# Second mixer's gate and branch slabs computed token-major, with 512 moving weight columns

## The chip, the cores and the metric

One core of one Trainium2 chip runs the whole kernel. The metric is the device time in microseconds of one execution, the median of three runs.

## What is computed

Two transformer blocks over 256 tokens of 1024 features, in fp32. The change touches the second block's mixer (`hybrid_mixer`): three branches of width 512 (stick-breaking attention `ya`, spatial gating `yb`, gated short convolution `yc`), each projected to 1024 features and weighted by a sigmoid gate that is itself a projection of the normed input; the weighted sum is projected once more.

```
p = h @ w_in                                   # h is the normed input, (256, 1024)
q, k, v, z, cb, cc, cx, gates = split(p)       # gates: 3 * 1024 columns
br = stack([ya, yb, yc], axis=2)               # (256, 3, 512)
br_d = einsum("bsnc,ncd->bsnd", br, w_branch)  # (256, 3, 1024)
g = sigmoid(gates.reshape(bsz, seq, 3, 1024))
merged = sum(g * br_d, axis=2)                 # (256, 1024)
return merged @ w_out
```

## The kernel before

All weights pass through a ring of four places in SBUF in slabs of 128 x 2048 words (1 MB). SyncE loads slab i when slab i-4 has been used (`slab_used`). Every fp32 product is made of three fp32r matmuls, high by high, high by low and low by high (`mm3`, lines 529 to 531). For this ScalarE copies each slab into `w_hi` (line 1065) and VectorE subtracts that to make `w_lo` (line 1502). Each engine has its own program in a fixed order, and semaphores tie them together. `hi(i)`, `lo(i)` and the waits stand in these programs exactly where they run.

`form_a` is feature-major: a 128x128 block of the weights is stationary, and the 256 tokens of the input move past it. The output has features on partitions and tokens along the free dimension. A slab of 256 columns and 8 blocks of input features takes 48 matmuls of 256 columns. `form_b_half` is token-major: a 128x128 block of the input is stationary and 512 weight columns move. The output has tokens on partitions. A slab of 4 blocks of input features and 512 columns takes 24 matmuls of 512 columns. Both forms are in use in the kernel before.

The mixer's stage takes slabs 87 to 104 in six rounds r = 0 to 5, one for each branch (order `yb`, `yc`, `ya`) and half of the output features. A round has three slabs: two gate slabs and one branch slab. Round 0 is 87, 88 and 89, round 1 is 90, 91 and 92, and so on to 102, 103 and 104. Slabs 105 to 108 are the output projection (`form_b`), which is token-major and takes the merged result as features on partitions, split into `xh` and `xl` (lines 1408 and 2060). The PSUM banks `feat(0)` and `feat(1)` hold the gates, `feat(2)` and `feat(3)` the branch's output.

In a round of the kernel before, TensorE does the first gate slab into `feat(0)` and the second into `feat(1)`. VectorE multiplies each by the tokens' norm scales, which lie along the free dimension (`row_of_scales`, line 2069), into `sig2` in SBUF, and counts `gate_in`. TensorE of the next round waits for `gate_in` before it writes the bank anew. ScalarE makes the sigmoid in place (line 1421, `gate_ready`). After the branch slab VectorE merges: products of PSUM and `sig2` (lines 2088 and 2093) and a sum (line 2094), `merge_done`.

Beside these slabs run the steps of the stick-breaking attention, for four pairs of heads. TensorE does scores (line 917), sums (929 to 931) and values (939, 940) after fixed slabs (`beside`), and ScalarE (lines 1343 to 1355, with Exp and Ln) and VectorE (lines 1941 to 1967) serve them in their own queues (`early`, `beside`). In round 0 ScalarE's order is: exponential of pair 1, `hi` of slabs 90 and 91, the logarithm step of pair 2, and then the two sigmoids. Just before it stand the splits of `yb` and `yc` (lines 1401 and 1403), the latter waiting for VectorE's products at line 2050.

Of the kernel before, what the change touches and what calls it, by code (L numbers as in the profile page):

```python
# [158 lines left out]
def weight_count(i):  # L159

    return i + 1 if i < I_M2 else i


def build(nc, a, out):

    with ExitStack() as ctx:
# [3 lines left out]
        def at(name, shape, off, dt=F32):  # L170
            assert off + int(np.prod(shape[1:])) <= ARENA_WORDS, (name, off)
            return nc.alloc_sbuf_tensor_at(name, shape, dt, offset=ARENA + 4 * off)
# [101 lines left out]
        y3_pad = at("y3_pad", [P, 4, CONV3 - 1 + S], kv0)  # L274
        cc_s = at("cc_s", [P, 2, S], kv0 + 4 * (CONV3 - 1 + S))
        acc3 = at("acc3", [P, 4, S], kv0 + 4 * (CONV3 - 1 + S) + 2 * S)
        merged = at("merged", [P, KD, S], kv0)
        vg = at("vg", [P, TB, HALF], kv0 + 3 * D)
        sig2 = at("sig2", [P, 4, S], kv0 + 3 * D)
        y_h = [at("ya_h", [P, 4, S], xn0, F32R), at("yb_h", [P, 4, S], split0, F32R),  # L280
               at("yc_h", [P, 4, S], split0 + 2 * D, F32R)]
        y_l = [at("ya_l", [P, 4, S], xn0 + D, F32R), at("yb_l", [P, 4, S], split0 + D, F32R),
# [23 lines left out]
        def feat(b):  # L306
            return ps[:, 4 + b, :]

        def blocks(x):
            return x.rearrange("p (t n) -> p t n", n=S)  # L310

        def sem(name):
            return ctx.enter_context(nc.semaphore(name))
# [10 lines left out]
        gain_loaded, gain_used = sem("gain_loaded"), sem("gain_used")  # L324
        raw_t, raw_hi, raw_lo, hg_ready, h_scaled = sem("raw_t"), sem("raw_hi"), sem("raw_lo"), sem("hg_ready"), sem("h_scaled")
        diag_ready, row_t, row_ready = sem("diag_ready"), sem("row_t"), sem("row_ready")
        sig_in, rg_in, ug_in, gate_in, glu_in_ready = (sem(x) for x in ("sig_in", "rg_in", "ug_in", "gate_in", "glu_in_ready"))
        fill, const_ready, tables_ready, dist_set = sem("fill"), sem("const_ready"), sem("tables_ready"), sem("dist_set")
        ws_masked, pad3_ready = sem("ws_masked"), sem("pad3_ready")
        act_step, dve_step = sem("act_step"), sem("dve_step")  # L330
# [37 lines left out]
        def _(sp):  # L368
            def load(i, src, step=0, wait_step=0):

                s = PLACE[i]
                if BEFORE[i] is not None:
                    sp.wait_ge(slab_used, BEFORE[i] + 1 + wait_step)
                dst = w_ring[:, s, :].rearrange("p (k n) -> p k n", n=src.shape[2])
                sp.dma_start(dst, src).then_inc(w_loaded[s], 16)

            def panel_a(w, col, n=256):
                return w.rearrange("(k p) n -> p k n", p=P)[:, :, col:col + n]
# [61 lines left out]
            for n, br in enumerate(BRANCH_ORDER):  # L440
                for half in range(2):
                    i = I_BR + 6 * n + 3 * half
                    for j in range(2):
                        load(i + j, panel_a(w2, 8 * HALF + D * br + HALF * half + 256 * j))
                    load(i + 2, panel_a(wb[br], HALF * half, HALF))
            for j in range(4):
                load(I_OUT2 + j, rows_b_form(a["w_out_2"].squeeze(0), 256 * j))
# [77 lines left out]
        def _(pe):  # L525
# [427 lines left out]
            def beside(i):  # L953

                for step, p in SB_AT.get(i, ()):
                    step(p)
# [28 lines left out]
            mm.then_inc(sgu_mixed, 1)  # L985
            form_a(I_C3 + 5, (3,), x_t)
            beside(I_C3 + 5)
            for n, br in enumerate(BRANCH_ORDER):
                for half in range(2):
                    i = I_BR + 6 * n + 3 * half  # L990
                    r = 2 * n + half
                    if r == 0:
                        pe.wait_ge(yb_ready, 2)
                    for j in range(2):
                        if r > 0:
                            pe.wait_ge(gate_in, 2 * r - 1 + j)
                        form_a(i + j, (j,), x_t)
                        beside(i + j)
                    if r == 0:
                        pe.wait_ge(yc_ready, 2)  # L1000
                    else:
                        pe.wait_ge(merge_done, r)
                    pe.wait_ge((sb_lo, yb_lo, yc_lo)[br], (4, 1, 1)[br])
                    form_a(i + 2, (2, 3), (y_h[br], y_l[br]), n=HALF)
                    beside(i + 2)

            pe.wait_ge(sb_lo, 4)
            form_b(I_OUT2, x_t, range(4), lambda s: pe.wait_ge(merged_lo, 1 + s // 2),
                   lambda: raw_transpose(R_XA2, 0, UPD[I_OUT2]))
            raw_transpose(R_XA2, 1, UPD[I_OUT2])  # L1010
            x_attention(1, I_Q2, I_O2, raw_ready(R_XA2), lambda: raw_transpose(R_FF2, 0, UPD[I_O2]))
# [40 lines left out]
        def _(act):  # L1052
# [316 lines left out]
            def early(i):  # L1369

                for step, p in SB_EARLY.get(i, ()):
                    step(p)

            def beside(i):
                for step, p in SB_AT.get(i, ()):
                    step(p)
# [27 lines left out]

            def merged_split(half):

                act.wait_ge(merge_done, 5 + half)
                act.activation(xh[:, 4 * half:4 * half + 4, :], merged[:, 4 * half:4 * half + 4, :], ACT.Copy).then_inc(merged_hi, 1)

            for n in range(BRANCHES):  # L1410
                for half in range(2):
                    i = I_BR + 6 * n + 3 * half
                    r = 2 * n + half
                    if r == 0:
                        sb_exps(1)
                        hi(i + 3)
                        hi(i + 4)
                        sb_logs(2)
                    for j in range(2):
                        act.wait_ge(gate_in, 2 * r + j + 1)  # L1420
                        act.activation(sig2[:, 2 * j:2 * j + 2, :], sig2[:, 2 * j:2 * j + 2, :], ACT.Sigmoid).then_inc(gate_ready, 1)
                        if 0 < r < 5:
                            early(i + j)
                            hi(i + j + 3)
                            beside(i + j)
                    if r == 5:
                        merged_split(0)
                        hi(i + 3)
                        hi(i + 4)
                    early(i + 2)  # L1430
                    if r < 5:
                        hi(i + 5)
                    beside(i + 2)
# [55 lines left out]
        def _(dve):  # L1489
# [51 lines left out]
            def row_of_scales(n):  # L1541

                return r_row[:, n, :].unsqueeze(1).broadcast_to([P, 2, S])
# [438 lines left out]
            def early(i):  # L1982

                for step, p in SB_EARLY.get(i, ()):
                    step(p)
# [69 lines left out]
            dve.tensor_tensor(y_l[2][:, :, :], acc3[:, :, :], y_h[2][:, :, :].bitcast(F32), ALU.subtract).then_inc(yc_lo, 1)  # L2055

            def merged_split(half):
                dve.wait_ge(merged_hi, half + 1)
                f = slice(4 * half, 4 * half + 4)
                dve.tensor_tensor(xl[:, f, :], merged[:, f, :], xh[:, f, :].bitcast(F32), ALU.subtract).then_inc(merged_lo, 1)  # L2060


            for n in range(BRANCHES):
                for half in range(2):
                    i = I_BR + 6 * n + 3 * half
                    r = 2 * n + half
                    for j in range(2):
                        dve.wait_ge(slab_used, i + j + 1)
                        dve.tensor_tensor(sig2[:, 2 * j:2 * j + 2, :], blocks(feat(j)), row_of_scales(0), ALU.mult).then_inc(gate_in, 1)
                        if 0 < r < 5:  # L2070
                            early(i + j)
                            lo(i + j + 3)
                            beside(i + j)
                    if r == 0:
                        sb_masked(1)
                        lo(i + 3)
                        lo(i + 4)
                        sb_penalty(2)
                    if r == 5:
                        merged_split(0)  # L2080
                        lo(i + 3)
                        lo(i + 4)
                    dve.wait_ge(gate_ready, 2 * r + 2)
                    dve.wait_ge(slab_used, i + 3)
                    m = merged[:, 4 * half:4 * half + 4, :]
                    if n == 0:
                        for j in range(2):
                            ins = dve.tensor_tensor(m[:, 2 * j:2 * j + 2, :], blocks(feat(2 + j)), sig2[:, 2 * j:2 * j + 2, :], ALU.mult)
                            after(ins)
                    else:  # L2090
                        for j in range(2):
                            s2 = sig2[:, 2 * j:2 * j + 2, :]
                            after(dve.tensor_tensor(s2, blocks(feat(2 + j)), s2, ALU.mult))
                        after(dve.tensor_tensor(m, m, sig2[:, :, :], ALU.add))
                    dve.sem_inc(merge_done, 1)
                    early(i + 2)
                    if r < 5:
                        lo(i + 5)
                    beside(i + 2)
# [104 lines left out]
```

## Time and profile before

| what | us |
|---|---|
| median of three runs (lowest to highest) | 943.25 (943.23 to 944.71) |
| the profiled execution | 943.54 |
| its span, first to last instruction | 941.8 |
| TensorE matmul busy | 918.0 |
| TensorE weight load busy | 822.0 |
| VectorE busy | 672.5 |
| ScalarE busy | 486.8 |
| mean granted TensorE clock | 0.997 of full |

The profile is of one execution. Engines are PE (TensorE), PEld (its weight loads), DVE (VectorE), ACT (ScalarE), POOL (GpSimd) and SP (SyncE). Matmul ends are modelled and matmuls overlap, so the distance between starts tells what one costs. In brackets behind a row of a timeline stands the idle time of the engine before it, with what released it.

### The profile page before, as it was taken

What the parts mean: (1) busy time and instruction counts of PE and PEld (TensorE: products, weight loads), DVE (VectorE), ACT (ScalarE), POOL (GpSimd) and SP (SyncE); (2) the same over time, 40 slices, a digit from 0 to 9 for tenths busy, and PEclk for the clock granted to TensorE, in tenths of its full rate; (3) what the DMA queues carried; (4) which work ended last, traced back from release to release, by engine and by line L of the source; (5) the groups of instructions that cost most, each with busy time, mean ns of one, the idle gap of its engine ahead of it and who ended that gap; (6) DMA issues with size and microseconds to landing.
All of it is one profiled execution on the core that took longest, in us unless ns stands there. A gap on an engine that the chain in (4) does not pass through costs nothing.

```text
span 941.8 us, 14045 instructions
## 1 busy us (share of the span) xinstructions
PE 918.0 (97%) x5768; PEld 822.0 (87%) x5768; DVE 672.5 (71%) x964; ACT 486.8 (52%) x554; POOL 6.9 (1%) x37
## 2 busy tenths in 40 slices
PE   6998999999999999999999999999999999999996
PEld 6996999889888888888999999999898888888885
DVE  5799999888576566666866886765786676565665
ACT  6776435475455444445646546653564554544442
POOL 1000000000000000000000000000000000000000
PEclk9999999999999999999999999999999999999998
DMA  9675545454346655654755444545453455556551
GB/s 316 236 232 181 179 135 171 142 179 145 124 143 198 196 178 181 202 196 146 234 180 179 154 157 138 180 157 189 147 179 114 155 179 179 184 197 196 180 179 45
DMA packets 112467, 164.43 MB, mean 175 GB/s; under 512 B 2784, under 2 KB 90464, under 8 KB 112416
## 3 DMA queue, kind: packets, MB, share of 16 engines
q1 hardware_dynamic: 111856, 161.87, 52.6%
q0 software_dynamic: 560, 1.84, 0.6%
q8 instruction: 38, 0.62, 0.3%
q14 instruction: 13, 0.11, 0.0%
HBM read 162.64 MB, written 1.05 MB: 174 GB/s over the span
## 4 chain that ended last, share of the span: by engine, by line
PE 87%; DVE 9%; DMA 2%; ACT 2%; issue 1%; SPq 0%; DVEq 0%
PE ps L529 20%; PE ps L531 20%; PE ps L530 20%; PE ps L572 14%; PE ps L573 7%; DVE w_lo L1502 3%; DMA w_ring<-in_w_in 2%; DVE c_acc L1641 2%; PE ps L660 1%; PE ps L696 0%; ACT w_hi L1065 0%; DVE acc L2040 0%; DVE h L1560 0%; DVE mem_l L1517 0%; ACT c_out L1241 0%
## 5 line engine op out<-in xcount | busy, mean ns | idle before, releaser
L1502 DVE TENSOR_TENSOR w_lo<-w_ring,w_hi 128x2048 fp32r<-128x2048 f32 x147 | 335.5, 2289 | 122.1 <-ACT w_hi L1065 120.2
L1065 ACT ACTIVATE w_hi<-w_ring 128x2048 fp32r<-128x2048 f32 x147 | 279.9, 1908 | 80.0 <-DMA w_ring<-in_w_in 25.9
L572 PE MATMUL ps<-xx,w_hi 128*128 128x512 f32 x576 | 203.9, 398 | 0.3
L529 PE MATMUL ps<-xx,w_hi 128*128 128x256 f32 x616 | 177.3, 288 | 8.9 <-DVE w_lo L1597 8.7
L530 PE MATMUL ps<-xx,w_hi 128*128 128x256 f32 x616 | 175.2, 284 | 0.0
L531 PE MATMUL ps<-xx,w_lo 128*128 128x256 f32 x616 | 175.2, 284 | 0.0
L573 PE MATMUL ps<-xx,w_lo 128*128 128x256 f32 x576 | 161.6, 280 | 0.0
L572 PEld LDWEIGHTS ps<-xx,w_hi 128*128 128x128 f32 x576 | 108.2, 188 | 27.0 <-issue 0.7
L529 PEld LDWEIGHTS ps<-xx,w_hi 128*128 128x128 f32 x616 | 119.1, 193 | 10.6 <-DVE w_lo L1597 9.0
L530 PEld LDWEIGHTS ps<-xx,w_hi 128*128 128x128 f32 x616 | 119.2, 193 | 0.0
L531 PEld LDWEIGHTS ps<-xx,w_lo 128*128 128x128 f32 x616 | 119.1, 193 | 0.0
L573 PEld LDWEIGHTS ps<-xx,w_lo 128*128 128x128 f32 x576 | 108.7, 189 | 0.6
L529 PE MATMUL ps<-w_hi,ff_h 128*128 128x512 f32 x216 | 84.7, 392 | 0.0
L531 PE MATMUL ps<-w_hi,ff_l 128*128 128x512 f32 x216 | 84.3, 390 | 0.0
L530 PE MATMUL ps<-w_lo,ff_h 128*128 128x512 f32 x216 | 84.2, 390 | 0.0
L529 PE MATMUL ps<-w_hi,xx 128*128 128x512 f32 x192 | 75.9, 395 | 2.4 <-issue 1.5
L531 PE MATMUL ps<-w_hi,xx 128*128 128x512 f32 x192 | 74.9, 390 | 0.0
L530 PE MATMUL ps<-w_lo,xx 128*128 128x512 f32 x192 | 74.8, 390 | 0.0
L1641 DVE SCALAR_TENSOR_TENSOR c_acc<-u_pad,cols,c_acc 128x256 f32<-128x256 f32 x120 | 48.8, 478 | 0.2 <-DVE stat L1510 0.2
L531 PEld LDWEIGHTS ps<-w_hi,ff_l 128*128 128x128 f32 x216 | 40.5, 188 | 9.0
L529 PEld LDWEIGHTS ps<-w_hi,ff_h 128*128 128x128 f32 x216 | 40.5, 188 | 8.7 <-DVE ff_l L1879 0.2
L530 PEld LDWEIGHTS ps<-w_lo,ff_h 128*128 128x128 f32 x216 | 40.6, 188 | 7.9
(307 smaller groups left out, 1317.3 us busy)
## 6 DMA issues: line engine op xcount, KB each, us to landing
w_ring<-in_w_in SPq DMA_DIRECT2D x36, 1024.0 KB, 5.1
w_ring<-in_mlp_up_w SPq DMA_DIRECT2D x16, 1024.0 KB, 5.5
w_ring<-in_mlp_down_w SPq DMA_DIRECT2D x16, 1024.0 KB, 4.9
w_ring<-in_w_gate_ffn SPq DMA_DIRECT2D x11, 1024.0 KB, 5.3
w_ring<-in_w_up_ffn SPq DMA_DIRECT2D x11, 1024.0 KB, 5.3
w_ring<-in_w_down_ffn SPq DMA_DIRECT2D x11, 1024.0 KB, 4.9
w_ring<-in_xkv_w SPq DMA_DIRECT2D x8, 1024.0 KB, 5.3
w_ring<-in_w_out SPq DMA_DIRECT2D x8, 1024.0 KB, 4.9
```

What stands on the lines that cost most here:

```text
L529: pe.matmul(o, lh, rh, start=first, stop=False)
L530: pe.matmul(o, lh, rl, start=False, stop=False)
L531: return pe.matmul(o, ll, rh, start=False, stop=last)
L572: mm = pe.matmul(o, wh[:, k, c], xx[:, k, :, :].rearrange("p e t -> p (e t)"), start=k == 0, stop=False)
L573: mm = pe.matmul(o[:, 0:S], wl[:, k, c], xx[:, k, 0, :], start=False, stop=k == KD - 1)
L660: mm = pe.transpose(ps[:, bank, (k - k0) * P:(k - k0 + 1) * P], h[:, tb, k * P:(k + 1) * P], ident[:, :])
L1065: act.activation(w_hi[:, s, :], w_ring[:, s, :], ACT.Copy).then_inc(hi_done, 1)
L1502: dve.tensor_tensor(w_lo[:, s, :], w_ring[:, s, :], w_hi[:, s, :].bitcast(F32), ALU.subtract).then_inc(lo_done, 1)
L1641: ins = dve.scalar_tensor_tensor(c_acc[:, c, :], win, tap, c_acc[:, c, :], ALU.mult, ALU.add)
```

## The change

The gate slabs and the branch slabs of the six rounds go token-major. The gate slabs are loaded as 4 blocks of input features by 512 columns in place of 8 by 256, and TensorE runs them with `form_b_half` into `feat(0)` (tokens 0 to 127) and `feat(1)` (tokens 128 to 255). Both banks are complete only after the second gate slab. The branch slab has the branch's output as stationary operand. Since tokens now lie on partitions, the norm scale is a scalar for each partition, and ScalarE applies it within the sigmoid, straight from PSUM; VectorE's product and `gate_in` go. TensorE waits for `gate_ready` before the next round's gate slabs. ScalarE and VectorE prepare the next slabs ahead of the sigmoids in rounds 1 to 5. The merged result now has tokens on partitions, so TensorE turns it with eight transposes for each half, and the split into `xh` and `xl` reads PSUM in two pieces.

```
@@ buffers
-        merged = at("merged", [P, KD, S], kv0)
+        merged = at("merged", [P, TB, D], kv0)
-        sig2 = at("sig2", [P, 4, S], kv0 + 3 * D)
+        sig2 = at("sig2", [P, TB, HALF], kv0 + 3 * D)
@@ SyncE
                     for j in range(2):
-                        load(i + j, panel_a(w2, 8 * HALF + D * br + HALF * half + 256 * j))
+                        load(i + j, rows_b_form(w2, 512 * j, 8 * HALF + D * br + HALF * half, HALF, 4))
@@ TensorE
+            def merged_transpose(half, bank):
+
+                for k in range(4):
+                    for tb in range(TB):
+                        mm = pe.transpose(bank(k // 2)[:, (k % 2) * S + tb * P:(k % 2) * S + (tb + 1) * P],
+                                          merged[:, tb, half * HALF + k * P:half * HALF + (k + 1) * P], ident[:, :])
+                mm.then_inc(merged_t, 1)
...
                     if r == 0:
                         pe.wait_ge(yb_ready, 2)
-                    for j in range(2):
-                        if r > 0:
-                            pe.wait_ge(gate_in, 2 * r - 1 + j)
-                        form_a(i + j, (j,), x_t)
-                        beside(i + j)
+                    else:
+                        pe.wait_ge(gate_ready, 2 * r)
+                    form_b_half(i, 4, x_t, lambda: beside(i))
+                    beside(i + 1)
                     if r == 0:
                         pe.wait_ge(yc_ready, 2)
                     else:
                         pe.wait_ge(merge_done, r)
                     pe.wait_ge((sb_lo, yb_lo, yc_lo)[br], (4, 1, 1)[br])
-                    form_a(i + 2, (2, 3), (y_h[br], y_l[br]), n=HALF)
+                    if r == 5:
+                        merged_transpose(0, tok)
+                    pe.wait_ge(lo_done, weight_count(i + 2))
+                    wh, wl = slab(i + 2, HALF)
+                    for kk in range(4):
+                        for tb in range(TB):
+                            t = slice(tb * P, (tb + 1) * P)
+                            mm = mm3(feat(2 + tb), (y_h[br][:, kk, t], y_l[br][:, kk, t]), (wh[:, kk, :], wl[:, kk, :]), kk == 0, kk == 3)
+                    mm.then_inc(slab_used, 1)
                     beside(i + 2)

+            def merged_ready(s):
+
+                if s == 1:
+                    pe.wait_ge(merge_done, 6)
+                    merged_transpose(1, feat)
+                pe.wait_ge(merged_lo, 1 + s // 2)
+
@@ ScalarE
             def merged_split(half):

-                act.wait_ge(merge_done, 5 + half)
-                act.activation(xh[:, 4 * half:4 * half + 4, :], merged[:, 4 * half:4 * half + 4, :], ACT.Copy).then_inc(merged_hi, 1)
+                act.wait_ge(merged_t, half + 1)
+                for j in range(2):
+                    k = 4 * half + 2 * j
+                    act.activation(xh[:, k:k + 2, :], blocks((tok, feat)[half](j)), ACT.Copy).then_inc(merged_hi, 1)
...
-                    for j in range(2):
-                        act.wait_ge(gate_in, 2 * r + j + 1)
-                        act.activation(sig2[:, 2 * j:2 * j + 2, :], sig2[:, 2 * j:2 * j + 2, :], ACT.Sigmoid).then_inc(gate_ready, 1)
-                        if 0 < r < 5:
-                            early(i + j)
-                            hi(i + j + 3)
-                            beside(i + j)
+                    else:
+                        early(i)
+                        hi(i + 3)
+                        beside(i)
+                        early(i + 1)
+                        if r < 5:
+                            hi(i + 4)
+                        beside(i + 1)
+                    used_slab(i + 1)
+                    if r > 0:
+                        act.wait_ge(merge_done, r)
+                    for tb in range(TB):
+                        act.activation(sig2[:, tb, :], feat(tb), ACT.Sigmoid, scale=r_mix2[:, tb:tb + 1]).then_inc(gate_ready, 1)
                     if r == 5:
                         merged_split(0)
-                        hi(i + 3)
                         hi(i + 4)
@@ VectorE
-                    for j in range(2):
-                        dve.wait_ge(slab_used, i + j + 1)
-                        dve.tensor_tensor(sig2[:, 2 * j:2 * j + 2, :], blocks(feat(j)), row_of_scales(0), ALU.mult).then_inc(gate_in, 1)
...
-                    if r == 5:
-                        merged_split(0)
+                    else:
+                        early(i)
                         lo(i + 3)
+                        beside(i)
+                        early(i + 1)
+                        if r == 5:
+                            merged_split(0)
                         lo(i + 4)
+                        beside(i + 1)
```

## Rows read from the trace of the kernel before

**Rows 1.** Page: TensorE's busy line, and the chain that ended last by engine.
```profile
PE 918.0 (97%) x5768; PEld 822.0 (87%) x5768; DVE 672.5 (71%) x964; ACT 486.8 (52%) x554; POOL 6.9 (1%) x37
...
PE 87%; DVE 9%; DMA 2%; ACT 2%; issue 1%; SPq 0%; DVEq 0%
```

**Rows 2.** Windows, TensorE: from:to, length, busy (matmuls), clock, DMA share, GB/s.
```profile
627.00:655.00 28.00, 28.00 (x235) 1.00 0.58 188
```

**Rows 3.** Timeline, TensorE, slabs 77 to 80: start us, length us, engine, line, operation.
```profile
483.40 0.28 PE L529 MATMUL ps<-xx,w_hi 128*128 128x256 f32 x1
...
494.91 0.40 PE L529 MATMUL ps<-w_hi,xx 128*128 128x512 f32 x1
...
505.59 0.39 PE L531 MATMUL ps<-w_hi,xx 128*128 128x512 f32 x1
```

**Rows 4.** Timeline, TensorE: first matmuls of slabs 88, 89 and 90, scores between.
```profile
554.85 0.39 PE L529 MATMUL ps<-xx,w_hi 128*128 128x256 f32 x1 [0.20 <-DVE w_lo L1502]
...
560.80 0.71 PE L917 MATMUL ps<-qkT 64*128 64x256 f32 x4
...
561.66 0.39 PE L529 MATMUL ps<-yb_h,w_hi 128*128 128x256 f32 x1
...
567.51 0.28 PE L529 MATMUL ps<-xx,w_hi 128*128 128x256 f32 x1
```

**Rows 5.** Timeline, ScalarE, round 0.
```profile
558.23 1.06 ACT L1403 ACTIVATE yc_h<-acc 128x1024 fp32r<-128x1024 f32 x1 [8.09 <-DVE acc L2050]
...
561.35 3.71 ACT L1065 ACTIVATE w_hi<-w_ring 128x2048 fp32r<-128x2048 f32 x2
...
567.94 0.84 ACT L1345 ACTIVATE sb_l<-sb_e 128x768 f32<-128x768 f32 x1
568.80 1.28 ACT L1421 ACT_TABLE_LOAD   x1
570.10 1.15 ACT L1421 ACTIVATE sig<-sig 128x512 f32<-128x512 f32 x2
```

**Rows 6.** Timeline, VectorE, the product that ScalarE waits for in rows 5.
```profile
557.51 0.68 DVE L2050 TENSOR_TENSOR acc<-ps,acc 128x512 f32<-128x512 f32 x1
```

**Rows 7.** Timeline, ScalarE: a table function from PSUM with a scale.
```profile
506.02 1.27 ACT L1393 ACTIVATE vg<-ps,stat 128x512 f32<-128x512 f32 x2 [4.08 <-PE ps L531]
```

**Rows 8.** DMA issues between 555 and 700 us: count, size, median us to landing.
```profile
w_ring<-in_w_in SPq DMA_DIRECT2D x8, 1024.0 KB, 5.1
```

**Rows 9.** Groups, VectorE, 546 to 690 us: busy us, mean ns | idle before.
```profile
L2069 DVE TENSOR_TENSOR sig<-ps,r_row 128x512 f32<-128x512 f32 x12 | 8.2, 686 | 5.9 <-PE ps L531 5.9
...
L2094 DVE TENSOR_TENSOR merged<-merged,sig 128x1024 f32<-128x1024 f32 x4 | 4.9, 1226 | 0.1
```

**Rows 10.** Chain that ended last: eight transposes of h.
```profile
680.40 0.87 PE ps L660 x8
```

**Rows 11.** Timeline, TensorE: last matmul of slab 104, first of slab 105.
```profile
661.28 0.28 PE L531 MATMUL ps<-ya_h,w_lo 128*128 128x256 f32 x1
662.43 0.47 PE L529 MATMUL ps<-w_hi,xx 128*128 128x512 f32 x1 [0.86 <-DVE w_lo L1502]
```

**Rows 12.** Timeline, TensorE: three matmuls of its first microseconds and its last one.
```profile
8.30 0.58 PE L529 MATMUL ps<-xx,w_hi 128*128 128x256 f32 x1 [8.30 <-DVE w_lo L1597]
...
13.82 0.41 PE L531 MATMUL ps<-xx,w_lo 128*128 128x256 f32 x1
...
14.20 0.28 PE L530 MATMUL ps<-xx,w_hi 128*128 128x256 f32 x1
...
933.30 0.39 PE L531 MATMUL ps<-w_hi,ff_l 128*128 128x512 f32 x1
```

**Rows 13.** Windows, all engines: PE, PEld, DVE, ACT, POOL busy, then clock, DMA, GB/s.
```profile
935.00:936.00 1.00, 0.00 (x0) 0.00 (x0) 0.97 (x2) 0.53 (x1) 0.00 (x0) 0.85 0.67 250
936.00:937.00 1.00, 0.00 (x0) 0.00 (x0) 0.83 (x5) 0.20 (x2) 0.00 (x0) 0.50 0.00 0
```

**Rows 14.** Waits of TensorE: in total us, times, longest us.
```profile
PE ps L645 <- ACT w_ring L1078: 1.8, 1, 1.8
```

More of the change, by code:

```diff
@@ L326, in build @@
         diag_ready, row_t, row_ready = sem("diag_ready"), sem("row_t"), sem("row_ready")
-        sig_in, rg_in, ug_in, gate_in, glu_in_ready = (sem(x) for x in ("sig_in", "rg_in", "ug_in", "gate_in", "glu_in_ready"))
+        sig_in, rg_in, ug_in, glu_in_ready = (sem(x) for x in ("sig_in", "rg_in", "ug_in", "glu_in_ready"))
+        merged_t = sem("merged_t")
         fill, const_ready, tables_ready, dist_set = sem("fill"), sem("const_ready"), sem("tables_ready"), sem("dist_set")
@@ L1003, in _ @@
                     pe.wait_ge((sb_lo, yb_lo, yc_lo)[br], (4, 1, 1)[br])
-                    form_a(i + 2, (2, 3), (y_h[br], y_l[br]), n=HALF)
-                    beside(i + 2)
+                    if r == 5:
[7 more added lines that the diff above has]
+                    mm.then_inc(slab_used, 1)
+                    beside(i + 2)
+            def merged_ready(s):
[3 more added lines that the diff above has]
+                pe.wait_ge(merged_lo, 1 + s // 2)
             pe.wait_ge(sb_lo, 4)
-            form_b(I_OUT2, x_t, range(4), lambda s: pe.wait_ge(merged_lo, 1 + s // 2),
+            form_b(I_OUT2, x_t, range(4), merged_ready,
                    lambda: raw_transpose(R_XA2, 0, UPD[I_OUT2]))
@@ L2057, in merged_split @@
             def merged_split(half):
-                dve.wait_ge(merged_hi, half + 1)
-                f = slice(4 * half, 4 * half + 4)
-                dve.tensor_tensor(xl[:, f, :], merged[:, f, :], xh[:, f, :].bitcast(F32), ALU.subtract).then_inc(merged_lo, 1)
+                for j in range(2):
+                    k = 4 * half + 2 * j
+                    dve.wait_ge(merged_hi, 2 * half + j + 1)
+                    ins = dve.tensor_tensor(xl[:, k:k + 2, :], blocks((tok, feat)[half](j)), xh[:, k:k + 2, :].bitcast(F32), ALU.subtract)
+                ins.then_inc(merged_lo, 1)
             for n in range(BRANCHES):
@@ L2066, in _ @@
                     r = 2 * n + half
-                    for j in range(2):
-                        dve.wait_ge(slab_used, i + j + 1)
-                        dve.tensor_tensor(sig2[:, 2 * j:2 * j + 2, :], blocks(feat(j)), row_of_scales(0), ALU.mult).then_inc(gate_in, 1)
[L2070 to L2073, printed above, removed]
                     if r == 0:
@@ L2078, in _ @@
                         sb_penalty(2)
-                    if r == 5:
-                        merged_split(0)
+                    else:
+                        early(i)
                         lo(i + 3)
+                        beside(i)
+                        early(i + 1)
+                        if r == 5:
+                            merged_split(0)
                         lo(i + 4)
+                        beside(i + 1)
                     dve.wait_ge(gate_ready, 2 * r + 2)
                     dve.wait_ge(slab_used, i + 3)
[L2085 to L2088, printed above, removed]
+                    m = merged[:, :, half * HALF:(half + 1) * HALF]
+                    for tb in range(TB):
+                        o = m[:, tb, :] if n == 0 else sig2[:, tb, :]
+                        ins = dve.tensor_tensor(o, feat(2 + tb), sig2[:, tb, :], ALU.mult)
+                        if n or tb:
                             after(ins)
[L2090 to L2093, printed above, removed]
+                    if n:
                         after(dve.tensor_tensor(m, m, sig2[:, :, :], ALU.add))
```

## Prediction

> **What bounds the kernel now.** I read the page first. TensorE is busy 97% of the span and carries 87% of the chain that ended last [rows 1]. That average says nothing of one stage, so I took the busy time of TensorE over 28 us in the middle of the changed stage: 28.00 of 28.00 us [rows 2]. In the timeline of TensorE the stage from slab 87 to slab 104 has one matmul behind another, and the only holes are 0.20 us before slab 88 and 0.86 us before slab 105, both put down to w_lo. So a change shows on the clock there only by what it takes from TensorE's own stream or by the waits it puts into it. VectorE and ScalarE stand idle for much of these rounds, and what they save is worth nothing unless TensorE waits for it.
>
> The length of a matmul in the trace (0.28 or 0.39 us) is not its price: they overlap. The price is the distance between starts. From 483.40 to 494.91 lie 96 matmuls of 256 columns: 11.51 / 96 = 0.120 us. From 494.91 to 505.59 lie 47 steps of 512-column matmuls of the same token-major kind: 10.68 / 47 = 0.227 us [rows 3].
>
> **Part 1: 512 moving columns.** A slab had 48 matmuls of 256 columns, 48 x 0.120 = 5.76 us. It will have 24 of 512 columns, 24 x 0.227 = 5.45 us. That is 0.31 us a slab on TensorE, 5.5 us over 18 slabs, if nothing else ends last. The Trainium skill's page "TensorE: Matmul & The Clock Gate", section "Back-to-back issue gap", prices the step as columns / 2.4 plus 2.5 ns; an estimate by that page is 5.24 against 5.18 us a slab, 1.1 us in all. The measured steps disagree with it (0.120, not 0.109), and the sum goes by them.
>
> Not all of it arrives. Slab 88 starts at 554.85 behind a w_lo that VectorE ends at that moment [rows 4], and VectorE's queue before it waits for steps that the change doesn't touch. So what slab 87 saves is absorbed. Slab 88 starts at 554.85 again, the scores take the 0.86 us from 560.80 to 561.66 [rows 4], and slab 89 would start near 561.35 and its matmuls would be issued by 566.9, where before the next slab began at 567.51 [rows 4].
>
> **Part 2: the wait that takes the place of the old one.** Before, slab 90 (the first gate slab of round 1) waited only until VectorE had copied the gates of round 0 out of PSUM. Now ScalarE reads them itself, and TensorE waits on gate_ready for both sigmoids of round 0. What is queued ahead of them on ScalarE in round 0: the split of yc (558.23), a table load and the exponential of pair 1, two w_hi (561.35, 3.71 us), the logarithm step of pair 2 (its Ln at 567.94), the load of the sigmoid's table (568.80, 1.28 us), and then the two sigmoids, 570.10 to 571.25 [rows 5]. None of this moves up: its head waits for VectorE's second product at 557.51 [rows 6], at the end of a dense VectorE stretch that hangs on slab 86. The VectorE products that are removed come behind it. A table function read from PSUM with a scale costs as much as one from SBUF: two Gelu of that form took 1.27 us [rows 7]. So the sigmoids end at about 571.25 as before, and slab 90 starts at about 571.35, with 0.05 to 0.1 us lost on a first matmul. Against 567.51 that is 3.9 us late. TensorE stands idle from the end of slab 89 (about 567.0) for 4.3 us. Behind the waiting instruction everything on TensorE is queued, and through slab_used also SyncE's loads, but these have room.
>
> **Part 3: slabs 90 to 104.** 15 slabs x 0.31 = 4.6 us back. I followed the three queues through rounds 1 to 5 for more waits. In a later round the sigmoids stand behind w_hi of slab i+4, whose load is issued when gate slab i is used and lands 5.1 us later [rows 8]; then w_hi 1.9, a table load 1.28 where Exp or Ln came between, and two sigmoids 1.2 us [rows 5]. That ends 8.2 to 9.5 us after gate slab i. TensorE asks for it after the second gate slab, the branch slab and the attention steps beside them, 11.7 us or more after it. Some 2 us of room in the tightest rounds (2 and 3), more elsewhere. The attention steps, which ScalarE and VectorE serve in the same queues, come after the same slabs as before. I price these waits at zero; the cover is those 2 us.
>
> **Part 4: VectorE's share.** Twelve products of 0.69 us go (8.2 us), and the merge keeps its length: two products of that same shape and one sum of 1.23 us [rows 9]. It is hidden behind a 5.45 us gate slab. Worth nothing by itself.
>
> **Part 5: turning the result.** Eight 128x128 transposes cost TensorE 0.87 us where h is turned [rows 10]. There are two such groups, before slab 104 and before slab 106: 1.7 us on TensorE's stream. The reads of the first turn by ScalarE and VectorE (two of 0.6 and two of 0.69 us) lie beside slab 104, those of the second beside slab 106, which needs nothing of them; slab 107 does. In exchange the old hole goes: TensorE stood from 661.28 to 662.43 instead of one step, 1.03 us, because w_hi and w_lo of slab 105 came behind the split of the merged half [rows 11]. Now slab 105 is split two slabs earlier.
>
> **Part 6: the clock.** In this trace the granted clock fell once after work. TensorE's last matmul started at 933.30 and ended by 933.7 [rows 12]; the granted clock is 0.85 over 935 to 936 and 0.50 after it [rows 13], so it fell about 2.0 us after TensorE went idle. At the beginning, matmuls of 256 columns last 0.41 us up to 13.82 and 0.28 from 14.20 on, though the first was at 8.30 [rows 12]: 5.8 us at the lower level (1.2 of 2.4 GHz) before it rose. No idle time of TensorE between these is longer than 1.8 us [rows 14]. The new stall of 4.3 us is, so I expect the clock to fall in it and slab 90 to run its first matmuls at the lower level. Bounds: 0 if it doesn't fall, and half of 5.8 us, 2.9, if it stays low as long as at the start with dense matmuls. At the start 22 matmuls lost 0.095 us each, 2.1 us, in a stretch with waits in it. I take 1.7, a little under this nearest row, because the matmuls come dense. The same page of the Trainium skill, section "HAM oscillation — how this bites in real kernels", says that a wait between bursts throws the clock back and the next burst begins slow. By that rule this change pays twice for its stall; the end of the trace agrees.
>
> **Sum.** +3.9 (stall) - 4.6 (15 slabs) + 1.7 (transposes) - 1.0 (old hole) = 0.0, and with +1.7 (clock) +1.7 us. The profiled execution took 943.54 us (span 941.8, 1.7 around it), so it gives 945.2. The median of the three runs is 943.25, 0.3 lower; I predict against it: 944.9, with an own range of 943.8 to 946.4 from the clock's bounds and some 0.4 us of error in the stall.
>
> **The rivals.**
> A, stall without the clock's fall: the granted clock stays at 1.00 and only the even sum is left, 943.2 us. For it: the fall was seen once only, at the end of the program. Chance 0.18.
> B, slower: the wait for the sigmoids recurs in rounds 2 to 4. Place: gate_ready before slabs 96, 99 and 102. It decides from the point where landing, w_hi, table load and sigmoids together take 2 us longer than summed above, that is a load landing after more than 7.1 us or one more table load with its queueing. Price: a microsecond or so each over three rounds, 944.9 + 2.5 = 947.4. Against it: loads in this stage land in 5.1 us with the DMA engines 0.58 busy [rows 2, 8]. Chance 0.13.
> C, faster: the stall isn't there, since ScalarE reaches the sigmoids by 567. Then the slabs' 4.6 and slab 89's 0.6 stay, less 0.7: 938.8 us; with half the stall, no clock loss and 941. Against it: ScalarE's queue is in order and every step in it is in the trace. Chance 0.10.
> That TensorE's steps come out as the page's formula has them would cost 3.7 more (948.6); the measured steps leave it 0.01, counted in B.
>
> **How the numbers follow.** Forecast 0.59, A 0.18, B 0.13, C 0.10. About 0.2% (1.9 us) is what a measurement of this kernel can tell from no change: 941.4 to 945.1. The forecast lies 0.2 us inside this edge: I give 0.34 of its 0.59 to "same" and 0.25 to slower. With A that makes same 0.52, with B slower 0.38, with C faster 0.10. The 80% range leaves out C's far part and B's upper half: 941.8 to 947.4.
>
> **What would show it.** Steps of 0.227 us in all 18 slabs, none of 0.120. TensorE idle for 4.3 us before slab 90, released by ScalarE's sigmoid, its longest idle time after the start. The granted clock under 1.00 in the microseconds around it, and matmuls of more than 0.39 us at the head of slab 90. No idle before slabs 93, 96, 99 and 102. Transposes of 0.8 to 0.9 us before slabs 104 and 106, and no hole before slab 105. Wrong would be: sigmoids of round 0 well before 571 us, idle before other gate slabs, or a clock at 1.00 throughout.

## The result

Over seven runs each, the changed kernel takes 946.65 us (945.07 to 947.55) and the kernel before 943.98 us (943.17 to 944.71): ratio 1.0028, 95% interval 1.0017 to 1.0039. The change makes the kernel 2.7 us slower.

The page of the changed kernel has fewer instructions and a TensorE as busy as before [rows 1]: busy line, and the chain by engine.

```profile
span 945.3 us, 13205 instructions
...
PE 916.5 (97%) x5352; PEld 801.4 (85%) x5352; DVE 665.6 (70%) x954; ACT 487.6 (52%) x556; POOL 6.9 (1%) x37
...
PE 84%; DVE 9%; DMA 3%; ACT 2%; issue 2%; SPq 0%; DVEq 0%
```

TensorE's waits say where to look: whom it waited for, us in total, times, longest.

```profile
PE ps L530 <- DVE w_lo L1628: 8.6, 2, 8.4
PE ps L530 <- ACT sig L1457: 4.3, 1, 4.3
PE ps L530 <- DVE w_lo L1533: 3.2, 4, 1.8
```

The second line is new. It is one wait of TensorE, for the sigmoids of a round, and it is there once in six rounds. The timeline of TensorE shows it between slab 89 and slab 90 (compare rows 4), and what happens behind it:

```profile
567.58 0.39 PE L531 MATMUL ps<-w_lo,yb_h 128*128 128x512 f32 x1
567.80 0.39 PE L532 MATMUL ps<-w_hi,yb_l 128*128 128x512 f32 x1
572.50 0.50 PE L530 MATMUL ps<-w_hi,xx 128*128 128x512 f32 x1 [4.31 <-ACT sig L1457]
...
573.53 0.61 PE L531 MATMUL ps<-w_lo,xx 128*128 128x512 f32 x1
573.94 0.63 PE L532 MATMUL ps<-w_hi,xx 128*128 128x512 f32 x1
...
576.50 0.61 PE L532 MATMUL ps<-w_hi,xx 128*128 128x512 f32 x1
576.93 0.41 PE L530 MATMUL ps<-w_hi,xx 128*128 128x512 f32 x1
```

Before the wait the starts are 0.227 us apart. One microsecond after it they are 0.43 apart and a matmul lasts 0.63 us. The eight steps from 573.53 to 576.93 take 3.40 us where eight of 0.227 take 1.82, so 1.6 us are lost. The windows show the granted clock at its lower level (0.50) in just that stretch (columns as in rows 13):

```profile
572.00:573.00 1.00, 0.50 (x2) 0.46 (x3) 1.00 (x2) 0.45 (x1) 0.00 (x0) 1.00 0.69 266
573.00:574.00 1.00, 1.00 (x5) 0.77 (x5) 0.89 (x2) 0.00 (x0) 0.00 (x0) 0.77 0.00 0
574.00:575.00 1.00, 1.00 (x4) 0.80 (x3) 0.00 (x0) 0.00 (x0) 0.00 (x0) 0.50 0.06 16
...
576.00:577.00 1.00, 1.00 (x4) 0.73 (x3) 0.00 (x0) 0.00 (x0) 0.00 (x0) 0.52 0.00 0
577.00:578.00 1.00, 1.00 (x6) 0.83 (x5) 0.00 (x0) 0.00 (x0) 0.00 (x0) 1.00 0.00 0
```

ScalarE's queue in round 0 answers rows 5. It is the same queue, and its table function from PSUM takes what rows 7 had, 0.1 us more than the two sigmoids in place took before (1.26 against 1.15):

```profile
559.31 1.06 ACT L1427 ACTIVATE yc_h<-acc 128x1024 fp32r<-128x1024 f32 x1 [8.08 <-DVE acc L2081]
...
562.43 3.71 ACT L1089 ACTIVATE w_hi<-w_ring 128x2048 fp32r<-128x2048 f32 x2
...
569.89 1.28 ACT L1457 ACT_TABLE_LOAD   x1
571.18 1.26 ACT L1457 ACTIVATE sig<-ps,stat 128x512 f32<-128x512 f32 x2
```

All of it is 1.1 us later than in rows 5. So is TensorE from slab 86 on (541.24 against 540.15), and this shift arises in the first 90 us, where the two programs are the same and the waits for the first loads differ from one execution to the next. In the twelve profiled executions of this case the same step of TensorE starts anywhere between 87.9 and 88.9 us. So the shift isn't the change's. With it taken off, the sigmoids end within 0.1 us of the moment they had before, and the account of the two profiled executions, by the starts of the same steps on TensorE, reads:

| step | before | changed | difference | less the 1.1 |
|---|---|---|---|---|
| slab 88 | 554.85 | 555.93 | 1.1 | 0.0 |
| slab 89 | 561.66 | 562.43 | 0.8 | -0.3 |
| slab 90 | 567.51 | 572.50 | 5.0 | 3.9 |
| slab 105 | 662.43 | 664.50 | 2.1 | 1.0 |
| scores of the cross attention | 698.08 | 701.50 | 3.4 | 2.3 |
| end of the span | 941.8 | 945.3 | 3.5 | 2.4 |

Between slab 105 and the scores come the second group of transposes and 0.6 us of a wait for q_l. Both are in the timeline of TensorE, together with the first group and the start of slab 105, which has no hole before it now (rows 11 had 0.86 us):

```profile
658.17 1.03 PE L994 MATMUL ps<-ident,merged 128*128 128x128 f32 x8
658.96 0.48 PE L530 MATMUL ps<-w_hi,ya_h 128*128 128x512 f32 x1
...
664.50 0.39 PE L530 MATMUL ps<-w_hi,xx 128*128 128x512 f32 x1
...
669.94 1.03 PE L994 MATMUL ps<-ident,merged 128*128 128x128 f32 x8
670.73 0.48 PE L530 MATMUL ps<-w_hi,xx 128*128 128x512 f32 x1
...
701.50 0.39 PE L530 MATMUL ps<-k_h,q_h 128*128 128x256 f32 x1 [0.44 <-DVE q_l L1858]
```

### The profile page after: what moved, and what is told of

Read it like the earlier page. It is cut to its first block, busy times and chain, and to the rows that moved or that the text cites. A ratio compares the mean times of both kernels' runs of the same rounds, so it can differ in the third digit from the quotient of the medians.

```text
span 945.3 us, 13205 instructions
## 1 busy us (share of the span) xinstructions
PE 916.5 (97%) x5352; PEld 801.4 (85%) x5352; DVE 665.6 (70%) x954; ACT 487.6 (52%) x556; POOL 6.9 (1%) x37
## 4 chain that ended last, share of the span: by engine, by line
PE 84%; DVE 9%; DMA 3%; ACT 2%; issue 2%; SPq 0%; DVEq 0%
PE ps L530 20%; PE ps L532 19%; PE ps L531 19%; PE ps L573 14%; PE ps L574 7%; DVE w_lo L1533 3%; DMA w_ring<-in_w_in 2%; DVE c_acc L1672 2%; PE ps L661 1%; DMA w_ring<-in_w_q_xa 1%; ACT w_hi L1089 1%; PE ps L697 0%; DVE acc L2071 0%; DVE h L1591 0%; DVE mem_l L1548 0%
## 5 line engine op out<-in xcount | busy, mean ns | idle before, releaser
L574 PE MATMUL ps<-xx,w_lo 128*128 128x256 f32 x576 | 161.6, 281 | 0.0
L573 PEld LDWEIGHTS ps<-xx,w_hi 128*128 128x128 f32 x576 | 108.2, 188 | 27.0 <-issue 0.7
L530 PE MATMUL ps<-xx,w_hi 128*128 128x256 f32 x424 | 122.4, 289 | 8.6 <-DVE w_lo L1628 8.6
L530 PE MATMUL ps<-w_hi,xx 128*128 128x512 f32 x288 | 114.6, 398 | 6.8 <-ACT sig L1457 4.3
L531 PE MATMUL ps<-xx,w_hi 128*128 128x256 f32 x424 | 120.8, 285 | 0.0
L532 PE MATMUL ps<-xx,w_lo 128*128 128x256 f32 x424 | 120.7, 285 | 0.0
L532 PE MATMUL ps<-w_hi,xx 128*128 128x512 f32 x288 | 113.0, 392 | 0.0
L531 PE MATMUL ps<-w_lo,xx 128*128 128x512 f32 x288 | 112.9, 392 | 0.0
L574 PEld LDWEIGHTS ps<-xx,w_lo 128*128 128x128 f32 x576 | 108.7, 189 | 0.6
L530 PEld LDWEIGHTS ps<-xx,w_hi 128*128 128x128 f32 x424 | 82.1, 194 | 9.5 <-DVE w_lo L1628 8.8
L531 PEld LDWEIGHTS ps<-xx,w_hi 128*128 128x128 f32 x424 | 82.3, 194 | 0.0
L532 PEld LDWEIGHTS ps<-xx,w_lo 128*128 128x128 f32 x424 | 82.2, 194 | 0.0
L530 PEld LDWEIGHTS ps<-w_hi,xx 128*128 128x128 f32 x288 | 54.5, 189 | 20.1 <-ACT sig L1457 4.7
L532 PEld LDWEIGHTS ps<-w_hi,xx 128*128 128x128 f32 x288 | 54.5, 189 | 11.6
L531 PEld LDWEIGHTS ps<-w_lo,xx 128*128 128x128 f32 x288 | 54.4, 189 | 10.6
```

Source lines behind the costliest of these rows:

```text
L530: pe.matmul(o, lh, rh, start=first, stop=False)
L531: pe.matmul(o, lh, rl, start=False, stop=False)
L532: return pe.matmul(o, ll, rh, start=False, stop=last)
L573: mm = pe.matmul(o, wh[:, k, c], xx[:, k, :, :].rearrange("p e t -> p (e t)"), start=k == 0, stop=False)
L574: mm = pe.matmul(o[:, 0:S], wl[:, k, c], xx[:, k, 0, :], start=False, stop=k == KD - 1)
```

## The experiments

Each was timed in turns with the kernel before, on the same chip. The reference points are the medians of that kernel in the same comparison (943.7 to 943.9).

**The wait alone.** The kernel before, and only the wait added.

```diff
                         if r > 0:
                             pe.wait_ge(gate_in, 2 * r - 1 + j)
+                        if r == 1 and j == 0:
+                            pe.wait_ge(gate_ready, 2)
```

> The kernel before with one wait more: TensorE waits for both sigmoids of round 0 before slab 90. Nothing else differs. Theory (the new wait is the loss, and the clock falls in it): slab 90 starts at about 571.4 instead of 567.5, 3.8 us late, and the granted clock goes to its lower level for a few microseconds, 1.7 us more: about 5.5 us slower than before, 949.5. Rival (stall without clock): 3.8 us slower, 947.8, clock at 1.00. Rival (something else in the changed kernel costs the time): under 2 us slower.

Measured: 949.9 against 943.86 us, ratio 1.0061 (1.0047 to 1.0075), 6.0 us slower. TensorE starts slab 90 at 572.33 after 3.69 us of idle time. The windows show the clock at its lower level longer than in the changed kernel, and beginning inside the wait, and slab 90's matmuls start 0.213 us apart:

```profile
573.11 0.41 PE L529 MATMUL ps<-xx,w_hi 128*128 128x256 f32 x1
573.32 0.41 PE L530 MATMUL ps<-xx,w_hi 128*128 128x256 f32 x1
```

```profile
570.00:572.00 2.00, 0.00 (x0) 0.00 (x0) 1.81 (x3) 1.99 (x3) 0.00 (x0) 0.67 0.97 324
572.00:573.00 1.00, 0.67 (x3) 0.70 (x4) 1.00 (x2) 0.23 (x1) 0.00 (x0) 0.50 1.06 358
...
576.00:577.00 1.00, 1.00 (x7) 1.00 (x6) 0.00 (x0) 0.00 (x0) 0.00 (x0) 0.50 0.00 0
577.00:578.00 1.00, 1.00 (x8) 1.00 (x8) 0.00 (x0) 0.00 (x0) 0.00 (x0) 0.75 0.00 0
```

Low from 570.7 to 577.5, with TensorE at work from 572.33. From the start of slab 90 to that of slab 92 it takes 16.5 us where it took 14.2 before: 2.3 us lost to the clock, and 3.9 to the wait. The one wait costs more than the whole change, so the rest of the change is a gain.

**The wait filled with matmuls.** The changed kernel; the wait stays, but TensorE works in it.

```diff
                     else:
+                        if r == 1:
+                            pe.wait_ge(sb_prob, 2)
+                            for m in range(17):
+                                pe.matmul(tok(3), xh[:, 0, 0:P], xx[:, m % KD, :, :].rearrange("p e t -> p (e t)"), start=True, stop=True)
                         pe.wait_ge(gate_ready, 2 * r)
```

> The changed kernel with 17 matmuls of 512 columns, whose result nobody reads, put ahead of the wait for the sigmoids of round 0. The wait stays as long, TensorE is busy in it. Theory (clock): the granted clock stays at 1.00 through slab 90, its matmuls start 0.227 us apart, and the kernel is 1.7 us faster than the changed one (0.28% over before): about 0.1% over before, 944.9. Rival (the clock costs nothing on the median): as the changed kernel, 946.6.

Measured: 944.51 against 943.86 us, ratio 1.0006 (0.9997 to 1.0015). Slab 90 starts at full speed, and the clock is at 1.00 from 560 to 590. It starts no earlier in its execution: the whole of this one is 0.5 us ahead of the changed kernel's since 88 us, and slab 90 with it:

```profile
567.44 4.01 PE L1008 MATMUL ps<-xx 128*128 128x512 f32 x17
571.93 0.50 PE L530 MATMUL ps<-w_hi,xx 128*128 128x512 f32 x1 [0.47 <-ACT sig L1461]
572.26 0.40 PE L531 MATMUL ps<-w_lo,xx 128*128 128x512 f32 x1
```

Useless work makes the changed kernel 2.1 us faster (946.65 to 944.51). The two profiles, with their different first 88 us taken off, differ by 2.2 us: 1.6 is the clock, between the starts of slabs 90 and 92 (15.35 against 13.75 us), and 0.6 is the wait for q_l, which the profile of the filled wait doesn't have. How the 2.1 between the medians splits isn't shown. The filled wait is rival A made real: with the wait and without the clock's fall the change comes out near even.

**The sigmoids earlier in ScalarE's queue.** Only the order in round 0 changes.

```diff
                         sb_exps(1)
                         hi(i + 3)
+                        used_slab(i + 1)
+                        sigmoids()
                         hi(i + 4)
                         sb_logs(2)
```

> The changed kernel with ScalarE's queue of round 0 in another order: exponential of pair 1, w_hi of slab 90, both sigmoids, then w_hi of slab 91 and the logarithm step. By the trace the sigmoids end near 566.9 (on the time axis of the changed kernel, where slab 89 ends at 568.2), before slab 89 does. Theory: no stall before slab 90, clock at 1.00; against the changed kernel 4.3 us and 1.7 us less: 940.6 against 944.0 before, ratio 0.9965. Rival (further waits or the transposes hold it): the logarithm step comes one table load later and a new wait appears at the sums after slab 91; ratio 0.999 or more.

Measured: 940.0 against 943.86 us, ratio 0.9960 (0.9946 to 0.9973): 6.6 us below the changed kernel and 3.9 below the one before. ScalarE's timeline has the sigmoids done 1.1 us before slab 90 can start, and TensorE's runs through:

```profile
561.87 1.90 ACT L1089 ACTIVATE w_hi<-w_ring 128x2048 fp32r<-128x2048 f32 x1
563.78 1.28 ACT L1431 ACT_TABLE_LOAD   x1
565.08 1.27 ACT L1431 ACTIVATE sig<-ps,stat 128x512 f32<-128x512 f32 x2
```

```profile
567.24 0.39 PE L532 MATMUL ps<-w_hi,yb_l 128*128 128x512 f32 x1
567.47 0.39 PE L530 MATMUL ps<-w_hi,xx 128*128 128x512 f32 x1
```

The logarithm step now needs one more table load and ends at 573.2, and nobody on TensorE waits for it. The clock is at 1.00 around slab 90; it fell elsewhere in this execution, near 79 us, which the last section takes up.

**Both w_hi first, then the sigmoids.** The same edit with `hi(i + 4)` ahead of the sigmoids.

> As the kernel with early sigmoids, but with both w_hi ahead of the sigmoids and only the logarithm step behind them. The sigmoids end at about 568.7 on the axis of the changed kernel, where slab 89 ends at 568.2. Theory: a stall of about 0.5 us remains, too short for the clock to fall: 0.5 us slower than the one with early sigmoids, about 941.1, ratio 0.997. If the clock falls on any wait whatever, it would be 2.2 us slower than that.

Measured: 941.1 us, ratio 0.9970 (0.9958 to 0.9982), 1.1 us above the early sigmoids. The 95% intervals of the two overlap, so the traces have to tell. TensorE's wait is 0.55 us before slab 90, and the clock stays at 1.00. Slab 90 starts 6.3 us after slab 89, where it took 5.6 with early sigmoids: the short wait costs 0.7 us, its length and a slower first matmul. Another 0.6 us is in this execution the same wait for q_l as in the changed kernel.

**A stall of middle length.** The changed kernel, with w_lo of slab 88 moved on VectorE ahead of a step that waits for ScalarE. The chain that leads to the sigmoids gets 2.3 us shorter.

```diff
                 if k == 0:
+                    lo(I_C3 + 7)
                     early(I_C3 + 5)
...
-                lo(I_C3 + 7 + j)
+                if j:
+                    lo(I_C3 + 8)
```

> The changed kernel as it is, with only w_lo of slab 88 moved forward on VectorE. The chain up to the sigmoids of round 0 starts 2.3 us earlier and slab 89 ends 0.65 us earlier, so the stall is 2.7 us instead of 4.3. Theory: sigmoids end 2.2 us earlier, and everything behind them: 946.65 - 2.2 = 944.4 if the clock still falls, ratio 1.0006; 942.8 (0.9988) if 2.7 us of idle time leave it at its upper level. I expect it to fall in part of the executions, so a median between the two and a wider spread than with the stall filled.

Measured: 942.86 against 943.7 us, ratio 0.9991 (0.9982 to 1.0000), with single runs from 941.53 to 944.25. In the profiled execution TensorE waited 2.77 us and the clock fell nonetheless:

```profile
566.05 0.39 PE L532 MATMUL ps<-w_hi,yb_l 128*128 128x512 f32 x1
569.22 0.80 PE L530 MATMUL ps<-w_hi,xx 128*128 128x512 f32 x1 [2.77 <-ACT sig L1457]
```

```profile
569.00:570.00 1.00, 0.78 (x2) 0.69 (x3) 1.00 (x3) 0.16 (x1) 0.00 (x0) 0.54 1.04 399
...
572.00:573.00 1.00, 1.00 (x5) 0.82 (x4) 0.00 (x0) 0.00 (x0) 0.00 (x0) 0.75 0.00 0
```

Of the eleven executions, four have a mean granted clock of 0.998 over the span (median 942.1 us) and seven have 0.996 or 0.997 (median 943.45), 1.3 us more. The mean also counts the idle end of the program, where the clock is at 0.50 for 2.9 to 6.1 us in the twelve profiles (0.0015 to 0.0032 of the mean). So 0.998 leaves no room for a second low stretch of 3.4 us, and 0.996 needs one, but where it lay is seen only in the profiled execution. That the same wait lets the clock fall in some executions and not in others, at 1.3 us, fits these figures and isn't shown by a trace.

**The wide form taken back.** Early sigmoids, with each 512-column matmul of the 18 slabs made as two of 256; layout, waits and transposes stay.

```diff
+            def mm3_halves(o, left, right, first, last):
+                for e, c in enumerate((slice(0, S), slice(S, 2 * S))):
+                    mm = mm3(o[:, c], left, [w[:, c] for w in right], first and e == 0, last and e == 1)
+                return mm
```

> The kernel with early sigmoids; each matmul with 512 moving columns in the 18 gate and branch slabs is made as two of 256, with the same stationary block twice: 48 matmuls a slab again, all else (layout, waits, transposes) the same. Theory (the step of 0.120 us against 0.227 us is what the wide form saves): 18 x 0.31 = 5.5 us less what the hole before slab 88 absorbs, 5.2 us slower than with early sigmoids: 945.2, ratio 1.0014. Rival (the page's formula, 0.06 us a slab): 1 us slower, 941, ratio 0.997.

Measured: 944.96 against 943.71 us, ratio 1.0009 (1.0000 to 1.0018), 5.0 us above the early sigmoids. With the first 88 us taken off, slab 88 starts at the same moment in both profiles, behind its w_lo, so 17 slabs carry the difference: 5.0 / 17 = 0.29 us a slab. The steps are again 0.12 us apart:

```profile
590.79 0.28 PE L532 MATMUL ps<-w_hi,xx 128*128 128x256 f32 x1
590.91 0.28 PE L530 MATMUL ps<-w_hi,xx 128*128 128x256 f32 x1
```

**The transposes twice.** Early sigmoids, and `for k in (*range(4), *range(4))` in `merged_transpose`.

> The kernel with early sigmoids, each of the two groups of eight transposes of the merged result run twice. Theory (the transposes lie fully on TensorE's path): two groups of 0.8 us more, 1.6 us slower than the one with early sigmoids, 941.6, ratio 0.9977. Rival (the waits around them hide them, or the splits behind them are late as well): 0.996 or above 0.999.

Measured: 941.18 against 943.7 us, ratio 0.9972 (0.9962 to 0.9981), 1.2 us above the early sigmoids (940.0). Expected were 1.6, and the two intervals overlap. The traces are clearer: from the first transpose to the next matmul a group of sixteen takes 1.66 and 1.67 us where a group of eight took 0.79, and all of that is still there when the scores of the cross attention start. The transposes lie on TensorE's path.

```profile
650.82 1.91 PE L994 MATMUL ps<-ident,merged 128*128 128x128 f32 x16
652.48 0.48 PE L530 MATMUL ps<-w_hi,ya_h 128*128 128x512 f32 x1
```

**VectorE's products put back.** Early sigmoids, with twelve unused products of 128x512 at the old places. They read SBUF, where the old ones read PSUM.

```diff
+                    def product(j):
+                        dve.wait_ge(slab_used, i + j + 1)
+                        dve.wait_ge(yb_lo, 1)
+                        after(dve.tensor_tensor(ug[:, 2 * j:2 * j + 2, :], row_of_scales(0), row_of_scales(0), ALU.mult))
```

> The kernel with early sigmoids, with twelve products of 128x512 put back on VectorE at the old places (they wait for the same slabs, and read SBUF; their result isn't used). Theory (VectorE's share is hidden): no difference, 940.0, ratio 0.996. Rival (VectorE's relief is part of the gain): up to 8 us, seen as a ratio above 0.998.

Measured: 939.88 us, ratio 0.9958 (0.9945 to 0.9972), the same as without them. VectorE's 8.2 us were worth nothing that these runs can tell.

**Both orders mended.** Early sigmoids and w_lo of slab 88 moved.

> The kernel with early sigmoids, and on VectorE w_lo of slab 88 moved ahead of its wait for ScalarE's split of pair 0, into an idle stretch of 3.3 us. Theory: the hole of 0.65 us before slab 88 goes and what slab 87 saves arrives, nothing else is late: 0.6 to 0.9 us below the one with early sigmoids, about 939.3, ratio 0.9953. Rival (slab 89 or the sigmoids end last then): no difference from it, 0.996.

Measured: 938.49 (938.3 to 939.22) against 943.7 us, ratio 0.9948 (0.9934 to 0.9961). TensorE's timeline has no hole before slab 88; its first matmul comes right behind the sums:

```profile
553.94 0.39 PE L932 MATMUL ps<-sb_m,later 128*128 128x128 f32 x2
554.09 0.48 PE L530 MATMUL ps<-w_hi,xx 128*128 128x512 f32 x1
```

This has the lowest median of all versions: 5.2 us below the kernel before, 8.2 below the changed one. It is 1.5 below the early sigmoids, with intervals that overlap; the two profiles, with the first 88 us taken off, differ by 0.9.

**The moved w_lo alone, in the kernel before.**

> The kernel before with only w_lo of slab 88 moved forward on VectorE. Theory: the hole of 0.39 us before slab 88 goes and nothing else moves: 0.4 us faster, 943.4, ratio 0.9996. If it gave 1.5 us or more, as it adds to the one with early sigmoids, then that gain had nothing to do with the wide form.

Measured: 943.46 against 943.71 us, ratio 0.9998 (0.9989 to 1.0007): no difference that can be measured, as little as its 0.4 us hole. In the changed kernel the same edit was worth 3.8 us between the medians. There it shortens the new wait: slab 90 starts 2.5 us earlier in the profile, with the first 88 us taken off.

## Why the prediction was right

The forecast was 944.9 us, 1.7 above before, in a range of 941.8 to 947.4; measured are 2.7 above. The mechanism was the one forecast. By the forecast's own edge of 945.1 the outcome is "slower", which had 0.38 where "same" had 0.52, because the forecast lay 0.2 us inside the edge.

By the starts of the same steps in the two profiles, with the different first 90 us taken off, the terms are:

| term | forecast | profile |
|---|---|---|
| stall before slab 90 | +3.9 | +3.9 |
| 15 slabs | -4.6 | -4.3 |
| two groups of transposes | +1.7 | +1.6 |
| old hole before slab 105 | -1.0 | -1.0 |
| clock | +1.7 | +1.6 |
| wait for q_l | none | +0.6 |
| sum | +1.7 | +2.4 |

- **What bounds the stage:** right. Putting 8.2 us of work back on VectorE changed nothing, and the wait for the sigmoids showed in the time.
- **Part 1, 0.31 us a slab:** right in kind. The steps are 0.227 us, but over whole slabs, first matmuls and attention steps included, 0.29 us came back. The formula in the Trainium skill's page "TensorE: Matmul & The Clock Gate", section "Back-to-back issue gap", which the page gives for a matmul by itself and not for a stream of them, comes as an estimate to 1.1 us for all slabs; taking the wide form back cost 5.0.
- **Slab 87's saving absorbed:** right. Slab 88 started 0.0 us earlier than before, behind a w_lo hole that had grown from 0.20 to 0.46 us.
- **Part 2, the stall:** right, 4.3 us forecast and 4.31 found, slab 90 3.9 us late. The wait alone in the kernel before cost 3.9 of that and the clock. The table function from PSUM costs 0.1 us more than the one in place, where the forecast called them equal.
- **Part 3, later rounds:** right. No wait before slabs 93, 96, 99 and 102. Rival B didn't occur.
- **Part 5, transposes and the old hole:** right, two groups of 0.79 us to the next start, and the hole before slab 105 is gone.
- **Part 6, the clock:** right that it falls, and 1.7 us was close to the profiled 1.6. Against the forecast it fell not in the stall but 1.0 us behind it: the first four matmuls of slab 90 ran at full speed. The forecast set this stall apart from earlier waits of up to 1.8 us; two other profiles show a fall behind a wait of that length (last section). The price varies: the wait alone lost 2.3. Two of the changed kernel's seven executions, the median one among them, have a mean granted clock of 0.993 where the profiled one has 0.997, so they spent longer at the lower level, and no trace shows where.
- **The wait for q_l:** the forecast had nothing for it. It stands before the cross attention's scores. VectorE's queue was there behind w_hi and w_lo of slab 111, whose load came late: the four loads of that weight landed in 5.8 us at the median, against 5.3 before. Of the twelve profiled executions three have an idle time there, 0.44, 0.51 and 0.24 us (the changed kernel, "both w_hi first" and "products put back"), and they are the three in which these loads took 5.6 us or more; in the other nine they took 5.4 or less. The filled wait has the same code there as the changed kernel and no such wait. In these profiles it goes with the landing time, which differs between executions of the same order of work (the early sigmoids, without the wait, had 5.2); whether the change makes late landings more frequent isn't shown.

The filled wait checks the even sum of 0.0: its median is 0.65 us above before, and its profile, with the first 88 us taken off, 0.2. The remaining 0.3 us between the profiles' 2.4 and the medians' 2.7 is less than what the first 90 us alone differ by from one execution to the next.

Rival C named the fast case as "the stall isn't there", 938.8 us. It was wrong about this change, whose queue was as read, but its price is what the reordered versions measured: 940.0 with the hole before slab 88, and 938.49 without.

## What to carry to other kernels

When a step moves from one engine to another, read the new engine's queue around it: what counted here was what stood in front of the sigmoids once in six rounds. In the changed kernel slab 88 ended at 561.7 and the sigmoids' table load began at 569.9, 8.2 us of queued work later, and before the change TensorE did not wait for the sigmoids. A wait of a few microseconds on a TensorE that is otherwise dense costs its length and then, where the clock falls, some 2 us more at the lower level (1.6 and 2.3 here), so its removal can be worth more than its row in the waits shows. Fewer, wider matmuls on the same data save real time (0.29 us in 5.8 a slab), but a single badly placed wait eats eighteen slabs of it.

## What the runs showed of the hardware

The fall of the clock doesn't have to lie in the idle time that leads to it. In the changed kernel TensorE's last matmul ended at 568.2 and the next started at 572.50 at full speed; the granted clock fell at about 573.5, when TensorE was already at work, 5.3 us after it went idle. With the wait alone it fell inside the wait, about 2 us after TensorE went idle, as at the end of the kernel before [rows 13]. It stayed low for 3.4 us in the one and 6.8 us in the other. At the end of the program, behind the last matmul, the fall came 2.0 to 5.3 us after TensorE went idle in the twelve profiled executions. The Trainium skill's page "TensorE: Matmul & The Clock Gate", section "HAM oscillation — how this bites in real kernels", has the rule that the burst behind a wait starts slow. The end of the kernel before, which the forecast took as agreeing, shows the fall but no burst behind it. The wait alone and the 2.77 us wait agree with it: there the clock was down when slab 90 began. In the changed kernel the burst started fast and slowed down in its fifth matmul.

The length of a wait doesn't settle whether the clock falls. Near 77 us TensorE waits for a w_lo, in seven of the profiled executions for 1.8 us. In five of them the clock stayed at 1.00. In the early sigmoids and in the products put back it fell, 0.5 and 0.2 us after TensorE was at work again, and stayed low for 3.4 us. Here the early sigmoids, where the steps go from 0.227 to 0.43 us:

```profile
78.67 0.47 PE L530 MATMUL ps<-w_hi,mem_h 128*128 128x512 f32 x1 [1.83 <-DVE w_lo L1538]
...
79.64 0.63 PE L530 MATMUL ps<-w_hi,mem_h 128*128 128x512 f32 x1
80.06 0.63 PE L531 MATMUL ps<-w_lo,mem_h 128*128 128x512 f32 x1
```

```profile
79.00:80.00 1.00, 1.00 (x4) 0.83 (x3) 1.00 (x3) 0.21 (x2) 0.00 (x0) 0.60 0.88 352
80.00:81.00 1.00, 1.00 (x4) 0.74 (x3) 1.00 (x4) 0.00 (x0) 0.00 (x0) 0.50 0.97 397
```

It cost these executions little: TensorE's next wait, 1.8 us long at 84 us in the others, was down to 0.2 us. Where a wait follows, the lower clock only fills it; before slab 90 none followed.

The 0.55 us wait left the clock at its upper level in the profiled execution. The price of a wait is therefore not a constant: 1.6 us beyond its length in the profiled execution of the changed kernel, 2.3 with the wait alone.

The clock's rows don't cover the start of the program. They read 1.00 over the first 14 us of the kernel before, where matmuls of 256 columns last 0.41 us [rows 12], as they do at 0.50 in the profile of the wait alone. There the level has to be read from the matmuls.
